# Norm behind the per-layer gate in two pairs of token tiles, the gate's last six chunks tile by tile, all sigmoids ahead of one table load

## The reference

```python
def rmsnorm(x, g):
    xf = x.astype(jnp.float32)
    y = xf * lax.rsqrt(jnp.mean(xf * xf, axis=-1, keepdims=True) + RMS_EPS)
    return (y * g.astype(jnp.float32)).astype(x.dtype)
...
    for i in range(DEPTH):
        h = rmsnorm(x, g_mix[i])
        u = h @ w_in[i]
        ...
        ple_gate = jax.nn.sigmoid(rmsnorm(x, g_ple[i]) @ w_ple_gate[i])
        x = x + (p[i] @ w_ple[i]) * ple_gate
    return rmsnorm(x, g_final)
```

## Time and profile before

| | us |
|---|---|
| median of 3 runs | 2418.5 |
| lowest, highest | 2417.97, 2419.7 |
| profiled execution, its span | 2413.7 |
| PE busy in the span | 2291.1 |
| DVE, ACT, POOL busy | 1001.5, 586.5, 410.1 |

### The profile page before, as it was taken

The page is one execution under the profiler, slowest core; times in us unless marked ns, Lnnn a source line. Parts: engine busy times, 40 slices in busy tenths (PEclk is TensorE's granted clock), DMA queues, the critical chain, the costliest instruction groups (busy, mean ns, idle before and its releaser), DMA issues. The chain is left out here.

```text
span 2413.7 us, 29799 instructions
## 1 busy us (share of the span) xinstructions
PE 2291.1 (95%) x11910; PEld 1701.3 (70%) x11910; DVE 1001.5 (41%) x1763; ACT 586.5 (24%) x1210; POOL 410.1 (17%) x407
## 2 busy tenths in 40 slices
PE   7989999997899989999999899999989999999998
PEld 6667788654457767688754447877768887888887
DVE  5545543511145454643521136445743435232234
ACT  3533401311133442410311115223540002000012
POOL 2011111122211101111122121111101211111111
PEclk9999999999999999999999999999999999999999
DMA  5114536799961202233899983333213332333321
GB/s 163 49 50 104 133 105 243 318 422 422 420 260 59 70 21 79 67 96 141 326 415 422 422 351 86 97 83 88 74 45 98 89 120 75 103 98 96 96 96 71
DMA packets 291930, 396.57 MB, mean 164 GB/s; under 512 B 32590, under 2 KB 232014, under 8 KB 274378
## 3 DMA queue, kind: packets, MB, share of 16 engines
q1 hardware_dynamic: 274880, 366.27, 42.4%
q0 software_dynamic: 11328, 16.81, 1.9%
q10 hardware_dynamic: 5578, 11.51, 1.8%
HBM read 388.98 MB, written 30.15 MB: 174 GB/s over the span
## 5 line engine op out<-in xcount | busy, mean ns | idle before, releaser
L146 PE MATMUL banks<-h_split,w_high 128*128 128x512 f32 x2624 | 825.8, 396 | 2.3 <-PEq L3331 1.7
L146 PEld LDWEIGHTS banks<-h_split,w_high 128*128 128x128 f32 x2624 | 480.9, 188 | 104.1 <-issue 8.2
L198 DVE TENSOR_TENSOR w_low<-w_raw,w_high 128x1024 fp32r<-128x1024 f32 (+1 forms) x264 | 316.9, 1200 | 500.2 <-POOL w_high L187 500.1
L187 POOL CAST w_high<-w_raw 128x1024 fp32r<-128x1024 f32 (+1 forms) x264 | 276.4, 1048 | 1451.8 <-PE banks L146 1327.3
L146 PE MATMUL banks<-h_split,w_low 128*128 128x512 f32 x1312 | 512.1, 390 | 0.0
L146 PEld LDWEIGHTS banks<-h_split,w_low 128*128 128x128 f32 x1312 | 246.2, 188 | 52.7
L146 PE MATMUL banks<-w_high,op_split 128*128 128x512 f32 x736 | 228.4, 390 | 1.4 <-DVE mg_part L1359 1.1
L2093 PE MATMUL banks<-expert_ring,ex_xsT 128*64 128x256 f32 x1408 | 172.6, 401 | 27.0 <-DMA expert_ring<-in_w_exp_up 25.6
L2093 PEld LDWEIGHTS banks<-expert_ring,ex_xsT 128*64 128x64 f32 x1408 | 102.8, 144 | 84.4 <-DMA expert_ring<-in_w_exp_up 28.4
L146 PEld LDWEIGHTS banks<-w_high,op_split 128*128 128x128 f32 x736 | 138.1, 188 | 31.9 <-DVE mg_part L1359 2.4
L146 PE MATMUL banks<-w_low,op_split 128*128 128x512 f32 x368 | 143.2, 389 | 0.0
(11 more groups left out here) (449 smaller groups left out, 2748.1 us busy)
## 6 DMA issues: line engine op xcount, KB each, us to landing
w_raw<-in_w_in SPq DMA_DIRECT2D x142, 512.0 KB, 3.9
expert_ring<-in_w_exp_gate SPq DMA_DIRECT2D x42, 1024.0 KB
expert_ring<-in_w_exp_up SPq DMA_DIRECT2D x42, 1024.0 KB
expert_ring<-in_w_exp_down SPq DMA_DIRECT2D x42, 1024.0 KB, 23.9
region<-in_w_exp_gate SPq DMA_DIRECT2D x22, 1024.0 KB
region<-in_w_exp_up SPq DMA_DIRECT2D x22, 1024.0 KB
region<-in_w_exp_down SPq DMA_DIRECT2D x22, 1024.0 KB
w_raw<-in_w_gu SPq DMA_DIRECT2D x44, 512.0 KB, 3.9
```

The costliest lines, as they stand in the source:

```text
L146: last = nc.tensor.matmul(out, left, right, start=(start and n == 0), stop=(stop and n == 2), skip_group_check=True)
L187: self.nc.gpsimd.tensor_copy(self.high[:, i % self.SPLIT, 0:n], self.raw[:, i % self.RAW, 0:n]).then_inc(self.high_ready, 1)
L198: self.nc.vector.tensor_tensor(self.low[:, i % self.SPLIT, 0:n], self.raw[:, i % self.RAW, 0:n], self.high[:, i % self.SPLIT, 0:n].bitcast ...
```

## The change

The gate's last three pieces (chunks 2 to 7 of the second half) are done tile by tile. ACT does the four squares of the first half behind sigmoid 3 as before, then sigmoid, square, sigmoid, square, sigmoid, square, sigmoid, the table load, and then the root of tiles 0 and 1. The norm is made in two pairs of tiles. The first pair's part (sums, root, reciprocal, scaling, transposes, high and low parts of 256 tokens, with three of the next stream's weight pieces between) is now written in `embed_per_layer`, as is the second pair's root and scaling. The attention multiplies the first pair's tiles with the first pieces, then turns the second pair and multiplies it. The `unread` matmuls are gone at both borders. The mean and epsilon are taken in the root instruction (`scale=1.0 / D, bias=EPS`).

```diff
-    def on_vector(self, dve):
-        nc, k, ss = self.nc, self.k, self.ss
-        dve.wait_ge(self.squares_done, 2 * NT)
-        nc.vector.tensor_tensor(ss, k.halves[:, 0, 0, :], k.halves[:, 0, 1, :], ALU.add).then_inc(self.summed, 1)
-        dve.wait_ge(self.summed, 1)
-        nc.vector.tensor_scalar(ss, ss, 1.0 / D, EPS, ALU.mult, ALU.add).then_inc(self.mean_ready, 1)
-        dve.wait_ge(self.root_ready, 1)
-        nc.vector.reciprocal(ss, ss).then_inc(self.rstd_ready, 1)
-        dve.wait_ge(self.rstd_ready, 1)
-        for t in (0, 1, 2):
-            nc.vector.tensor_scalar(self.xn[:, t, :], k.x[:, t, :], ss[:, t:t + 1], None, ALU.mult).then_inc(self.xn_dve, 1)
-        dve.wait_ge(self.gain_landed, 16)
...
+    def sums(self, dve, pair):
+        cols = slice(2 * pair, 2 * pair + 2)
+        dve.wait_ge(self.squares_done, NT + 2 * pair + 2)
+        self.nc.vector.tensor_tensor(self.ss[:, cols], self.k.halves[:, 0, 0, cols], self.k.halves[:, 0, 1, cols],
+                                     ALU.add).then_inc(self.summed, 1)
+
+    def root(self, act, pair):
+        cols = slice(2 * pair, 2 * pair + 2)
+        act.wait_ge(self.summed, pair + 1)
+        self.nc.scalar.activation(self.ss[:, cols], self.ss[:, cols], ACT.Sqrt, bias=EPS, scale=1.0 / D).then_inc(self.root_ready, 1)
+
+    def reciprocal(self, dve, pair):
+        cols = slice(2 * pair, 2 * pair + 2)
+        dve.wait_ge(self.root_ready, pair + 1)
+        self.nc.vector.reciprocal(self.ss[:, cols], self.ss[:, cols]).then_inc(self.rstd_ready, 1)
+        dve.wait_ge(self.rstd_ready, pair + 1)
...
+    def turn_pair(self, pe, pair):
+
+        wait(pe, self.low_done, DC * pair)
+        for t, landed in ((2 * pair, self.xn_dve), (2 * pair + 1, self.xn_act)):
+            pe.wait_ge(landed, pair + 1)
+            for c in range(DC):
+                bank, at = self.places[pair][c]
+                at += t % 2 * P
+                last = self.nc.tensor.transpose(self.k.ps[:, bank, at:at + P], self.xn[:, t, c::DC], self.k.ident[:])
+                if t % 2:
+                    last.then_inc(self.turned, 1)
+
+    def high_pair(self, act, pair, c):
+        bank, at = self.places[pair][c]
+        act.wait_ge(self.turned, DC * pair + (c | 1) + 1)
+        self.nc.scalar.activation(self.k.h[:, 0, c, pair * PAIR:(pair + 1) * PAIR], self.k.ps[:, bank, at:at + PAIR], ACT.Copy,
+                                  scale=self.g[:, c:c + 1]).then_inc(self.high_done, 1)
+
+    def low_pair(self, dve, pair, c):
+        bank, at = self.places[pair][c]
+        tokens = slice(pair * PAIR, (pair + 1) * PAIR)
+        dve.wait_ge(self.high_done, DC * pair + (c | 1) + 1)
+        self.nc.vector.scalar_tensor_tensor(out=self.k.h[:, 1, c, tokens], in0=self.k.ps[:, bank, at:at + PAIR],
+                                            scalar=self.g[:, c:c + 1], in1=self.k.h[:, 0, c, tokens].bitcast(F32), op0=ALU.mult,
+                                            op1=ALU.subtract).then_inc(self.low_done, 1)
+
+    def pair_split(self, pe, pair, c):
+        pe.wait_ge(self.low_done, DC * pair + c + 1)
...
-        for e in range(pieces - 2):
+        for e in range(pieces - st.SPLIT):
...
-        pe.wait_ge(st.low_ready, pieces)
+        first = DC - 2 * st.SPLIT
         for t in range(NT):
             tokens = slice(t * P, (t + 1) * P)
-            for c in range(DC // 2, DC):
+            for c in range(first, DC):
+                i = pieces - st.SPLIT + (c - first) // 2
+                if t == 0 and c % 2 == 0:
+                    pe.wait_ge(st.low_ready, i + 1)
                 last = split_product(nc, k.ps[:, NT + t, :], (k.h[:, 0, c, tokens], k.h[:, 1, c, tokens]),
-                                     st.part(pieces - 2 + (c - DC // 2) // 2, c % 2 * 512, 512), False, c == DC - 1)
-            (last.then_inc(tile_done, 1) if t < NT - 1 else last.then_inc(st.used, 2))
-        pe.wait_ge(sig_done, 1)
-        unread(k, 0, late.unread)
+                                     st.part(i, c % 2 * 512, 512), False, c == DC - 1)
+            (last.then_inc(tile_done, 1) if t < NT - 1 else last.then_inc(st.used, st.SPLIT))
+        late.turn_pair(pe, 0)
...
-            if i == 3:
-                for u in range(NT):
-                    late.square(act, u, 0)
-            if half and t:
-                late.square(act, t - 1, 1)
+
+        for i in range(NT):
+            gate(i)
+        for t in range(NT):
+            late.square(act, t, 0)
+        for t in (0, 1):
+            gate(NT + t)
+            late.square(act, t, 1)
+        gate(NT + 2)
+        late.square(act, 2, 1)
+        gate(NT + 3)
         act.preload_act_table_set("sqrt_and_others")
-        late.square(act, NT - 1, 1)
+        late.root(act, 0)
+        late.odd_tile(act, 0)
+        late.square(act, 3, 1)
+        act.wait_ge(late.gain_landed, 16)
+        for c in range(DC):
+            late.high_pair(act, 0, c)
+        late.root(act, 1)
+        late.odd_tile(act, 1)
...
-        for i in range(2 * NT):
+        for i in range(NT):
             gated(i)
-            if i == 1:
+            if i == 2:
                 st.split_low(dve, 7)
+        gated(NT)
+        gated(NT + 1)
+        late.sums(dve, 0)
+        late.stream.split_low(dve, 0)
+        late.stream.split_low(dve, 1)
+        gated(NT + 2)
+        late.reciprocal(dve, 0)
+        late.even_tile(dve, 0)
+        gated(NT + 3)
+        dve.wait_ge(late.gain_landed, 16)
+        for c in range(DC // 2):
+            late.low_pair(dve, 0, c)
+        late.stream.split_low(dve, 2)
+        for c in range(DC // 2, DC):
+            late.low_pair(dve, 0, c)
+        late.sums(dve, 1)
+        late.reciprocal(dve, 1)
+        late.even_tile(dve, 1)
...
+        for pair in range(PAIRS):
+            if pair:
+                norm.turn_pair(pe, pair)
+            for c in range(DC):
+                norm.pair_split(pe, pair, c)
+                st.rows(pe, VALUES + c // 4, c % 4, 4, c, lambda t: k.ps[:, t, 0:2 * P], tiles=(2 * pair, 2 * pair + 1))
+            for c in range(DC):
+                st.columns(pe, VALUES + 2, c, 4, slice(pair * PAIR, (pair + 1) * PAIR))
+        for j in range(1, 4):
```

162 lines of the change are left out of this document (88 added, 74 removed).

## The result

| kernel | median, us (lowest to highest) | profiled span, us | PE busy, us |
|---|---|---|---|
| before | 2418.32 (2417.20 to 2420.73) | 2413.7 | 2291.1 |
| after | 2425.73 (2424.58 to 2427.83) | 2422.8 | 2281.9 |

Six runs of each, on one chip: after takes 1.0031 times as long, 95% interval 1.0021 to 1.0041, that is 7.4 us more by the medians (5.1 to 9.9 by the interval). The forecast was 2422.5 (+4.0), its range 2417 to 2427. So the time is in the range, but the likeliest of the three cases, no measurable change, was the wrong one: the kernel is slower.

A forecast was written before the change was run, and what follows sets the result against it. TensorE, busy for 95% of the span, was taken as the bound. First border -1.3 + 0 + 1.7 = +0.4, second +4.4 - 0.8 = +3.6, together +4.0 us on a median of 2418.5: 2422.5 us, range 2417 to 2427.

The forecast's parts named there:

- the likeliest of the three cases, no measurable change: Time within 0.2% (4.8 us) of before; given a chance of 0.63, against slower 0.33 and faster 0.04.
- Part 1, piece 7: Gate's last weight piece comes late from DVE beside POOL's casts; PE stalls 0.9 us in first border, 4.9 in second.
- DVE taking turns with whole casts: By the skill's rule each DVE operation waits out a POOL cast, 1.7 us each; piece 7 0.4 us later.
- Part 2, first chain: First border, ACT and DVE work from gate to attention: first product at 761.7 us against 763.06, -1.3 us.
- Part 3, products of the first border: Attention products behind the first border, with one turn of 16 transposes, take 23.9 us as before: 0.
- Part 5, clock in the first border: Without unread products the clock falls; 3.4 us of first-border products run at half speed, +1.7 us.
- Part 4, second border: ACT and DVE queues bound the second border: first product 4.4 us later, products behind 0.8 us shorter, +3.6 us.
- a fall is in both kernels: Second border: the clock falls before and after the change alike, so no extra clock cost was charged there.
- the clock didn't stay up: Rival that the clock stays at full speed in the first border: 1.7 us less, 2420.8 us; chance 0.12.
- the plan didn't hold: Rival that piece 7 isn't late, DVE keeping its pace beside POOL: -4.2 us, 2414.3 us; chance 0.08.
- Long low clock: Rival that behind either border 5.9 us of products, not 3.4, run at 1.2 GHz: 2423.8 to 2425.5 us; chance 0.25.
- The rival's condition: The long low clock rival was to decide from 0.9 us of extra loss on.

The follow-up runs named there:

- e2: After, with 14 and 19 unread products put back ahead of the first transposes in the first and second border; ratio 1.0029.
- b1: Before, with its 17 and 25 unread products taken out and nothing else; ratio 1.0019.
- e6: After, with 19 unread products ahead of PE's wait for the gate's last piece, in the second border alone; ratio 1.0027.
- e1: After, with DVE subtracting the gate's piece 7 behind gated(1) instead of gated(2); ratio 1.0030.
- e3: After, with the next stream's first two weight pieces subtracted earlier on DVE, behind gated(4) and gated(5), ahead of the sums; one run, 2424.85 us.
- g4: g2 with 14 and 15 unread products, first pair's sums ahead of the third tile's multiply, its eight low parts ahead of the last tile's; ratio 0.9983.
- e4: After, with the edits of e1 and e3 together and 14 and 25 unread products; ratio 1.0001.
- b2: Before, unread products kept, with the gate's last three pieces done tile by tile; ratio 1.0013.
- g3: g2 with unread products and the gate's last three pieces, not two, tile by tile; ratio 0.9985.
- g2: After, two pieces tile by tile, piece 7 and weight splits earlier, ACT and DVE work reordered for the first pair, no unread products; ratio 0.9997.

## Why the prediction was right or wrong

**Part 1, piece 7:** right. PE's waits were 1.03 and 4.69 us (forecast 0.9 and 4.9), the three operations beside POOL took 4.33 us (4.4), the piece 1.21 (1.23). From the border's first sigmoid the piece was there at +11.4 us; by the rows it was to be at +11.5, by DVE taking turns with whole casts at +11.9 (the prediction's own 1.7 us, three times, are 0.7 above its 4.4, so it should have said +12.2). What the Trainium skill (SBUF — State Buffer, section SBUF: two separate sides) says of whole instructions would have given the later time. The trace has the turns, but shorter ones: operations and casts alternate one by one, and a pair of them takes 1.44 us (a third of 4.33; the three casts of 4.38 likewise), not the 1.7 that their lengths alone add up to.

**Part 2, first chain:** the order of waits was right, the gain wasn't. The last sigmoid was at +21.79 (forecast +21.66), but the first product at +29.00 instead of +27.86. Of this 1.1 us, 0.6 are the low clock in the transposes (e2: +28.39), and most of the other 0.5 the half-wide high and low part: from the high part's start to the product 1.47 us (760.82 to 762.29), where I took 1.04 from between 0.8 and 1.5.

```profile
760.82 2.66 ACT L477 ACTIVATE h_split<-banks,norm_g 128x256 fp32r<-128x256 f32 x7 [0.47 <-PE banks L470]
...
761.76 1.66 DVE L484 SCALAR_TENSOR_TENSOR h_split<-banks,norm_g,h_split 128x256 fp32r<-128x256 f32 x4 [2.17 <-ACT h_split L477]
```

The halves themselves were not slow: a high part starts every 0.36 us (seven in 2.66), where the full width has 0.58 (four in 2.42), and from low part to product it was 0.53 and not 0.80. What the forecast missed stands in the diff: `low_pair` waits for `(c | 1) + 1` high parts, so the first low part waits for two of them and starts 0.94 us behind the first. With a wait for one it would be some 0.6, and the term near the 1.04; that is an estimate from these rows, and wasn't run. The table load is 1.28 us with 0.02 until the root. The further 1.4 us of the Trainium skill (ScalarE: Activation LUTs, section What ACT_TABLE_LOAD costs) are not in this trace either.

**Part 3, products of the first border:** forecast 0, measured 24.8 against 23.9 us, +0.8. The second pair's turn and its wait took 2.73 us and not 2.1:

```profile
770.59 1.95 PE L470 MATMUL banks<-identity,region 128*128 128x128 f32 x16
773.32 0.50 PE L146 MATMUL banks<-w_high,h_split 128*128 128x512 f32 x1 [0.77 <-DVE h_split L484]
```

**Part 5, clock in the first border:** that it would fall was right, and b1 shows that the fillers had kept it up. The size failed: +1.7 for half-speed dense products, +0.6 measured, since the low clock, 3.4 us long as forecast, had ended (761.5) when the first product started (762.29), and slowed only the transposes. So the chain was off by +0.5, the clock by -1.1, the products by +0.8, and the border came out at +0.6 for a forecast of +0.4. This match is of errors that cancel, not of three right terms.

**Part 4, second border:** here the forecast failed, by 2.0 of 5.6 us. The first product was to be at +34.55 and was at +36.51. With the gap filled (e6) it was at +34.30: 2.2 us are the low clock in the gate. Of what is left, the last sigmoid came 0.8 earlier than reckoned (+26.99 for +27.80), and the low clock in the transposes cost 0.6: from last sigmoid to product 7.30 us, but 6.73 where fillers kept the clock up (e2), for a forecast of 6.75. So the chain of ACT and DVE was right, and what is missing is the clock, twice. The products behind took 20.8 us as forecast, but this again is of errors that cancel: the low clock cost them 0.6 and not 1.7; against that the second pair's turn and wait took 2.73 and not 2.1 (e2: 1522.49 to 1525.22), and the 144 half-wide products 17.5 and not 17.0. The step that failed is the sentence that in the second border a fall is in both kernels. It looked only at the products behind the border. There both kernels do have one, but it was 6.8 us long after and 3.4 before. And it took no account of the 4.9 us that Part 1 itself had made PE stand still, in the middle of the gate, with 13.6 us of dense products behind. The rows to price it were there: at 0.50 before, 0.5 us are lost for each us at the low clock. A stay with as much dense work in it as the one at 1349 us, 5.9 us, would have made it 3.0 on PE. Measured are 6.8 us at the low clock, 0.8 of them still in the gap; the gate's end was 2.7 us later than in e6, and the chain, which had waits of its own to give, 2.2.

**The rivals:** the clock didn't stay up, the plan didn't hold. "Long low clock" came out nearest in time (2423.8 to 2425.5 for 2425.7), and it is right that a low clock made the difference. It looked for it behind the borders. There the stay of the second was indeed longer (6.8 us for 3.4), but only 1.4 us of it lay on products; the larger part of the loss, 2.2 us, was in the gate. DVE didn't wait for whole casts. The rival's condition (over 0.9 us of extra loss) was met by the 2.0, so it is right in the number and in part in the cause.

**The total:** 6.2 us by the borders, 7.4 by the time. The 1.2 between them are within the interval (5.1 to 9.9), and nothing here says what they are.

## What to carry to other kernels

When you find that an edit makes TensorE wait, price the clock behind that wait too: ask in every gap of some us (4.7 us here; 1.2 us did nothing) what dense work follows, and reckon it at half speed, wherever the gap is. A gap that can't be removed can be filled, and filler in it is worth at most what the products behind it would lose (in e6 2.7 us at the gate's end, 2.2 behind the chain). And where two engines hand tiles to and fro, write down both queues for one tile and move out of the chain what the first consumer doesn't need; e1, e3 and g4 each gave about half of the wait that they removed, because the next was close behind.

## What the runs showed of the hardware

A gap of 4.7 us between dense matmuls was enough for the granted clock to fall to 1.2 GHz, in all three kernels that had it bare: in after at 1492.0 us (gap from 1488.1 to 1492.8), in e2 at 1488.3 (1484.7 to 1489.4), in e3 at 1494.3 (1490.6 to 1495.3). The waits of 1.2 us at the same place (e1, e4, b2, g3) didn't bring it down.

The stays at 1.2 GHz at the borders were 3.4, 6.8 or 10.2 us long, and nothing between. In the first border it fell 24.2 to 24.8 us behind the first sigmoid in all six kernels without filler there; it came back after 3.4 us in after, e6 and g2, after 6.8 in e1 and e3, after 10.2 in b1. After, e6 and e3 have the same chain up to that border's first product (+29.0 each), and yet the same work began again at +53.76, +53.79 and +54.71. What decides between the lengths is open; it makes the cost of one and the same gap differ by a us.

The second border of before, in which the clock fell in spite of 25 fillers, kept it at 1.00 in e2, in e4 and in each kernel of the new order with fillers. These turn 16 blocks and not 8 there, and their last wait ahead of the first product is 0.9 to 1.37 us, not 1.51. In b2, which has the 25 fillers, the 8 blocks and the 1.51 us, it fell. Which of the two did it wasn't tried.
